# Layout changes of u and y in a state-space stage: two DRAM round trips against transfers within on-chip memory

## The reference, cut to what matters

```python
u = (h @ w_in).reshape(B, S, G, C)             # 64 groups of 16 channels
# per group: 64 complex states, x[s] = a * x[s-1] + bbar @ u[s]
y = einsum(x_re, c_re) - einsum(x_im, c_im) + d_skip * u
y = gelu(y)                                    # tanh form
val, gate = split(y @ w_glu)
h = h + val * sigmoid(gate)
```

## Time and profile before

| what | value |
|---|---|
| median of 3 runs | 1100.39 us (1098.67 to 1102.09) |
| profiled execution | 1102.55 us |
| its span, first to last instruction | 1100.7 us |
| TensorE matmuls busy | 1086.2 us (99%) |
| VectorE busy | 785.0 us (71%) |
| ScalarE busy | 476.1 us (43%) |
| GpSimd busy | 63.1 us (6%) |
| mean granted TensorE clock | 0.996 of full |

### The profile page before, as it was taken

One profiled execution on the slowest core, in us unless ns is written; L12 is line 12 of the kernel. 1 busy time (PEld: TensorE's weight loads), 2 busy tenths in 40 slices (PEclk: granted clock), 3 DMA queues, 4 the chain that ended last, 5 costly groups with the idle time before them and its releaser, 6 DMA issues.

```text
span 1100.7 us, 15912 instructions
## 1 busy us (share of the span) xinstructions
PE 1086.2 (99%) x6180; PEld 891.6 (81%) x6180; DVE 785.0 (71%) x1171; ACT 476.1 (43%) x744; POOL 63.1 (6%) x162
## 2 busy tenths in 40 slices
PE   9999999999999999999999989999999999999997
PEld 6778878888888888888887778888888888888886
DVE  6869848688787788978868866557774467655765
ACT  6557734444324543345452223344442244413453
POOL 1383031000000000000000000000000000000000
PEclk9999999999999999999999989999999999999999
DMA  7332214233233333333287843222223233235622
GB/s 234 108 112 81 68 38 135 77 115 133 97 128 122 115 115 110 124 113 124 86 277 218 247 140 118 96 96 96 96 96 101 99 101 100 79 114 138 144 88 91
DMA packets 81546, 131.25 MB, mean 119 GB/s; under 512 B 39040, under 2 KB 49024, under 8 KB 81472
## 3 DMA queue, kind: packets, MB, share of 16 engines
q1 hardware_dynamic: 71856, 123.69, 35.4%
q0 software_dynamic: 1152, 4.19, 1.1%
q10 hardware_dynamic: 8464, 2.36, 0.9%
HBM read 111.02 MB, written 14.88 MB: 114 GB/s over the span
## 4 chain that ended last, share of the span: by engine, by line
PE 92%; DVE 3%; DMA 2%; DVEq 1%; issue 1%; ACT 1%; SPq 0%; ACTq 0%
PE bank L1774 27%; PE bank L1775 27%; PE bank L1776 27%; PE bank L1980 2%; DMA ud_scratch<-UB 2%; PE bank L2077 1%; PE bank L2079 1%; PE bank L2078 1%; PE bank L1965 1%; DMA YB<-yd_scratch 1%; PE bank L2044 1%; PE bank L1846 1%; PE bank L1955 0%; PE bank L1953 0%; PE bank L1952 0%
## 5 line engine op out<-in xcount | busy, mean ns | idle before, releaser
L614 ACT ACTIVATE WH<-RAW 128x1024 fp32r<-128x1024 f32 (+1 forms) x169 | 175.8, 1042 | 343.0 <-PE bank L1776 328.1
L1774 PE MATMUL bank<-GH,WH 128*128 128x512 f32 x816 | 320.7, 393 | 0.0
L1776 PE MATMUL bank<-GH,WL 128*128 128x512 f32 x816 | 317.7, 389 | 0.0
L1775 PE MATMUL bank<-GL,WH 128*128 128x512 f32 x816 | 317.5, 389 | 0.0
L1032 DVE TENSOR_TENSOR WL<-RAW,WH 128x1024 fp32r<-128x1024 f32 (+1 forms) x169 | 202.8, 1201 | 35.5 <-ACT WH L614 35.0
L1774 PE MATMUL bank<-AH,WH 128*128 128x512 f32 x532 | 209.1, 393 | 4.3 <-DVE AL L1561 3.4
L1776 PE MATMUL bank<-AH,WL 128*128 128x512 f32 x532 | 207.4, 390 | 0.0
L1775 PE MATMUL bank<-AL,WH 128*128 128x512 f32 x532 | 207.3, 390 | 0.0
L1774 PEld LDWEIGHTS bank<-GH,WH 128*128 128x128 f32 x816 | 153.1, 188 | 32.6 <-issue 0.7
L1776 PEld LDWEIGHTS bank<-GH,WL 128*128 128x128 f32 x816 | 153.2, 188 | 32.2
L1775 PEld LDWEIGHTS bank<-GL,WH 128*128 128x128 f32 x816 | 153.2, 188 | 31.9 <-issue 0.7
(11 more groups left out here) (299 smaller groups left out, 1050.1 us busy)
## 6 DMA issues: line engine op xcount, KB each, us to landing
RAW<-in_w_up SPq DMA_DIRECT2D x88, 512.0 KB, 3.3
RAW<-in_w_dn SPq DMA_DIRECT2D x32, 512.0 KB, 3.2
RAW<-in_w_glu SPq DMA_DIRECT2D x16, 512.0 KB, 3.3
RAW<-in_w_dn SPq DMA_DIRECT2D x16, 384.0 KB, 3.1
RAW<-in_w_wo SPq DMA_DIRECT2D x8, 512.0 KB, 3.4
od_scratch<-OO SPq DMA_DIRECT2D x8, 512.0 KB, 3.3
kd_scratch<-KT SPq DMA_DIRECT2D x8, 512.0 KB, 4.5
O<-od_scratch POOLq DMA_DIRECT2D x8, 512.0 KB, 6.4
```

Source lines behind the costliest of these rows:

```text
L614: act_(w_hi(b)[:, :n], RAW[b % RW][:, :n], ACT.Copy).then_inc(s_hi, 1)
L1774: mm(out, wh, hi_[:, k, :], start=start, stop=False)
L1775: mm(out, wh, lo_[:, k, :], start=False, stop=False)
L1776: return mm(out, wl, hi_[:, k, :], start=False, stop=stop)
```

## The change

u and y change layout by transfers from on-chip memory to on-chip memory. One u tile goes in eight transfers, one for each group of 16 partitions (32 KB each), from UB into U2, issued by SyncE; one y tile goes in eight transfers from Y2 into YB, issued by ScalarE. The DRAM tensors UD and YD and the transfers on SyncE that read them are gone.

The inputs of the projection, GH and GL, are written in (step, chunk) order as they are made in `next_tile`, and so is RSTD in `rstd_copy`; these now read with a stride, and the multiply that makes UB doesn't.

The tables of tiles 5 and 7 get places of their own over ET, the input matrices of the first four tiles, and wait for inputs that have been made (`s_E`) instead of outputs. Table loads come one step earlier on SyncE for tiles 4, 5 and 7. In the order of TensorE the first two GLU blocks do three units each before the next tile's inputs, and their fourth units follow together; on VectorE one `y_lo` goes ahead of the last `states`.

```diff
-LAGS_AT = {2: 4, 3: 3, 5: 5, 6: 7}
+LAGS_AT = {1: 4, 3: 3, 4: 5, 5: 7}
...
+        for j in (5, 7):
+            TM[j], _ = place(f"TM{j}", [P, 2 * QJ, C * LQ], F32, A0 + 4096 * (j - 5))
+            O2[j], _ = place(f"O2{j}", [P, 2, QJ, C * LQ], F32, A0 + 4096 * (j - 4))
...
+        def timed(x, kind):
+            return x.rearrange("p (k s) -> p s k", s=LQ) if kind == "mix1" else x
+        def chunked(x, kind):
+            return x.rearrange("p (s k) -> p s k", k=NK) if kind == "mix1" else x
+        def group(i):
+            return slice(C * i, C * i + C)
+        def u_landed(j):
+            return s_ur[j % 3], 16 * GJ * (j // 3 + 1)
+        def y_landed(j):
+            return s_yr[j % 2], 16 * GJ * (j // 2 + 1)
...
             def u_out(j):
                 sp.wait_ge(s_ev, nth(FIRST["win"] + j))
-                sp.dma_start(UD[j], UB[j % 2][:]).then_inc(s_uw, 16)
-            def u_in(j):
                 if j >= 3:
                     sp.wait_ge(s_Y, j - 2)
-                sp.wait_ge(s_uw, 16 * (j + 1))
-                sp.dma_start(U2[j % 3][:], cmaj(UD[j])).then_inc(s_ur[j % 3], 16)
-            def y_in(j):
-                if j >= 2:
-                    sp.wait_ge(s_act, TILE0["y"] + j - 1)
-                sp.wait_ge(s_yw[j % 2], 16 * (j // 2 + 1))
-                sp.dma_start(YB[j % 2][:], YD[j]).then_inc(s_yr[j % 2], 16)
+                for i in range(GJ):
+                    sp.dma_start(U2[j % 3][:, i, :], UB[j % 2][group(i)]).then_inc(s_ur[j % 3], 16)
...
-                act_(GH[:, j, :], X[:, j, :], ACT.Identity, scale=gain(kind, j)).then_inc(s_thi, 1)
+                act_(chunked(GH[:, j, :], kind), timed(X[:, j, :], kind), ACT.Identity, scale=gain(kind, j)).then_inc(s_thi, 1)
...
             def y_out(j):
                 act.wait_ge(s_g, j + 1)
-                nc.scalar.dma_start(cmaj(YD[j]), Y2[j % 2][:]).then_inc(s_yw[j % 2], 16)
+                if j >= 2:
+                    act.wait_ge(s_act, TILE0["y"] + j - 1)
+                for i in range(GJ):
+                    nc.scalar.dma_start(YB[j % 2][group(i)], Y2[j % 2][:, i, :]).then_inc(s_yr[j % 2], 16)
...
-                v.tensor_tensor(UB[j % 2][:], bank[BANK[b]][:].rearrange("p (k s) -> p s k", s=LQ),
-                                RSTD[:].rearrange("p (k s) -> p s k", s=LQ), ALU.mult).then_inc(s_ev, 1)
+                v.tensor_tensor(UB[j % 2][:].rearrange("p s k -> p (s k)"), bank[BANK[b]][:], RSTD[:],
+                                ALU.mult).then_inc(s_ev, 1)
...
             states(NJ - 2)
+            y_lo(NJ - 4)
             states(NJ - 1)
-            y_lo(NJ - 4)
...
-            glu_part((0,), range(4))
+            glu_part((0,), range(3))
             inputs(NJ - 2)
             outputs(NJ - 3)
-            glu_part((1,), range(4))
+            glu_part((1,), range(3))
+            glu_part((0, 1), (3,))
             inputs(NJ - 1)
             outputs(NJ - 2)
```

More of the change, by code:

```diff
@@ L324, in build @@
             O2[i], at = place(f"O2{i}", [P, 2, QJ, C * LQ], F32, at)
-        for j, i in ((3, 0), (5, 1), (7, 0)):
-            TM[j], O2[j] = TM[i], O2[i]
+        TM[3], O2[3] = TM[0], O2[0]
+        for j in (5, 7):
+            TM[j], _ = place(f"TM{j}", [P, 2 * QJ, C * LQ], F32, A0 + 4096 * (j - 5))
+            O2[j], _ = place(f"O2{j}", [P, 2, QJ, C * LQ], F32, A0 + 4096 * (j - 4))
         for j in (2, 4, 6):
@@ L348, in build @@
         KD_ = nc.dram_tensor("kd_scratch", (NJ, P, LQ, C * LQ), F32, kind="Internal").ap()
-        UD = nc.dram_tensor("ud_scratch", (NJ, P, LQ, NK), F32, kind="Internal").ap()
         TD = nc.dram_tensor("td_scratch", (3, P, P), F32, kind="Internal").ap()
-        YD = nc.dram_tensor("yd_scratch", (NJ, P, LQ, NK), F32, kind="Internal").ap()
         s_raw = [sem(f"raw{i}_loaded") for i in range(RW)]
@@ L375, in build @@
         s_tmr, s_or = [sem(f"TM{j}_loaded") for j in range(NJ)], [sem(f"O{j}_loaded") for j in range(NJ)]
-        s_uw, s_ur = sem("ud_written"), [sem(f"U{i}_loaded") for i in range(3)]
+        s_ur = [sem(f"U{i}_spread") for i in range(3)]
         s_rt, s_E, s_X, s_Y, s_g = sem("RT"), sem("E"), sem("states"), sem("Y"), sem("gelu")
-        s_yw, s_yr = [sem("even_yd_written"), sem("odd_yd_written")], [sem("YB0_loaded"), sem("YB1_loaded")]
+        s_yr = [sem("YB0_spread"), sem("YB1_spread")]
         s_sig = sem("sigmoid")
@@ L534, in _, with place_free @@
                         lags(j)
-            def u_out(j):
-                sp.wait_ge(s_ev, nth(FIRST["win"] + j))
-                sp.dma_start(UD[j], UB[j % 2][:]).then_inc(s_uw, 16)
-            def u_in(j):
-                if j >= 3:
-                    sp.wait_ge(s_Y, j - 2)
-                sp.wait_ge(s_uw, 16 * (j + 1))
-                sp.dma_start(U2[j % 3][:], cmaj(UD[j])).then_inc(s_ur[j % 3], 16)
-            def y_in(j):
-                if j >= 2:
-                    sp.wait_ge(s_act, TILE0["y"] + j - 1)
-                sp.wait_ge(s_yw[j % 2], 16 * (j // 2 + 1))
-                sp.dma_start(YB[j % 2][:], YD[j]).then_inc(s_yr[j % 2], 16)
+            def place_free(j):
+                if j == 3:
+                    sp.wait_ge(s_Y, 1)
+                if j in (5, 7):
+                    sp.wait_ge(s_E, j - 3)
             def lags_in(j):
@@ L554, in lags_in @@
                 sp.wait_ge(s_kw, 16 * (j + 1))
-                if j in PLACE_FREE:
-                    sp.wait_ge(s_Y, PLACE_FREE[j])
+                place_free(j)
                 sp.dma_start(TM[j][:], bass.AP(k.tensor, k.offset, [[C * LQ, P], [C * LQ * P, GJ], [1, C * LQ]])
@@ L565, in _, with u_out @@
             lags_in(2)
+            def u_out(j):
+                sp.wait_ge(s_ev, nth(FIRST["win"] + j))
+                if j >= 3:
+                    sp.wait_ge(s_Y, j - 2)
+                for i in range(GJ):
+                    sp.dma_start(U2[j % 3][:, i, :], UB[j % 2][group(i)]).then_inc(s_ur[j % 3], 16)
             for t in range(NJ):
                 u_out(t)
-                u_in(t)
-                if t >= 3:
-                    y_in(t - 3)
                 load(FIRST["win"] + 5 + t)
@@ L573, in _ @@
                     lags_in(LAGS_AT[t])
-            for j in range(NJ - 3, NJ):
-                y_in(j)
             def x_rows_in(n):
@@ L948, in gelu @@
                 if j >= 2:
-                    act.wait_ge(s_yw[j % 2], 16 * (j // 2))
+                    act.wait_ge(*y_landed(j - 2))
                 for gi in range(2):
@@ L1058, in rstd_copy @@
                 dve.wait_ge(s_bc, NORMS.index(norm) + 1)
-                v.tensor_copy(dst[:], bank[3][:]).then_inc(s_rstd, 1)
+                kind = "mix1" if norm == "n_dn02" else None
+                v.tensor_copy(chunked(dst[:], kind), timed(bank[3][:], kind)).then_inc(s_rstd, 1)
                 v.drain()
@@ L1300, in next_tile @@
                 dve.wait_ge(s_thi, TILE0[key] + j + 1)
-                v.scalar_tensor_tensor(out=GL[:, j, :], in0=X[:, j, :], scalar=gain(kind, j),
-                                       in1=GH[:, j, :].bitcast(F32), op0=ALU.mult,
+                v.scalar_tensor_tensor(out=chunked(GL[:, j, :], kind), in0=timed(X[:, j, :], kind), scalar=gain(kind, j),
+                                       in1=chunked(GH[:, j, :].bitcast(F32), kind), op0=ALU.mult,
                                        op1=ALU.subtract).then_inc(s_act, 1)
@@ L1522, in u_out @@
                 if j >= 2:
-                    dve.wait_ge(s_uw, 16 * (j - 1))
-                v.tensor_tensor(UB[j % 2][:], bank[BANK[b]][:].rearrange("p (k s) -> p s k", s=LQ),
-                                RSTD[:].rearrange("p (k s) -> p s k", s=LQ), ALU.mult).then_inc(s_ev, 1)
+                    dve.wait_ge(*u_landed(j - 2))
+                v.tensor_tensor(UB[j % 2][:].rearrange("p s k -> p (s k)"), bank[BANK[b]][:], RSTD[:],
+                                ALU.mult).then_inc(s_ev, 1)
             def states(j):
@@ L1760, in _ @@
             fetch(2)
-            pool.wait_ge(s_ur[2], 16)
+            pool.wait_ge(*u_landed(1))
             fetch(4)
-            for j in (3, 5, 7):
-                pool.wait_ge(s_Y, PLACE_FREE[j])
+            pool.wait_ge(s_Y, 1)
+            fetch(3)
+            for j in (5, 7):
+                pool.wait_ge(s_E, j - 3)
                 fetch(j)
@@ L2085, in inputs @@
             def inputs(j):
-                pe.wait_ge(s_ur[j % 3], 16 * (j // 3 + 1))
+                pe.wait_ge(*u_landed(j))
                 if j == 0:
```

5 lines of the change are left out of this document (1 added, 4 removed).

## The result

The changed kernel takes 1112.63 us (median, 1109.70 to 1113.19) against 1100.30 of the kernel before in the same rounds: 1.0112 of its time [1.0096, 1.0128], 12.3 us slower where 4.7 less were forecast. Its profiled run has a span of 1110.8 us, 10.1 more than before.

What follows compares the result with a forecast made beforehand. TensorE was taken as the bound, busy 1086.2 of 1100.7 us. Of 8.95 us recoverable, new waits take 4.3, leaving a gain of 4.65 from a median of 1100.39: forecast 1095.7 us, range 1091 to 1100.

Steps and rivals of the forecast that it cites:

- 8.95 us recoverable: State-space stage: three TensorE waits, 6.06 us together, plus 2.89 of lowered clock after the long one, all to be given back.
- rival 4: VectorE sets the pace and landings stay behind weight loads, so other waits replace the old ones whole: about 1100; 9%.
- The price of an issue: Each small transfer inside SBUF holds its issuing engine 0.63 us, so a tile's eight issues hold it 5.05 us.
- Rival 1: Issues cost only 0.37 to 0.43 us, nearly all new waits vanish: about 1092; 18%.
- rival 5: The small transfers don't overlap: eight by 2.1 us is 16.8 a tile against 8.79, about 1150; 2%.
- 2.66 + 5.05 = 7.7 still fits below 8.79: ScalarE's own work plus eight y issues fits one tile's TensorE period, in us; delay of the weights behind costed at nothing.
- rival 3: ScalarE's issues exceed what fits in a period, above 0.77 us each: about 1119 at 1.058 an issue; 13%.
- The four new waits, 4.3: TensorE late in the stage: 1.8 for the last u, 2.1 at the end, 0.2 each for u(6) and states(7).
- The order (step, chunk): Ahead of the stage, dearer strided GH and GL go into 4.4 us of slack, costing nothing; UB's multiply saves 0.42 a tile.
- The moved table: TM of tile 4, one step earlier ahead of u of tile 2 on SyncE: a wait costed at nothing up to 1 us.
- No clock loss: No new wait in the stage is as long as the 3.42 us one that lowered the clock, so none was counted.
- Rival 2: A new wait at the stage's end lowers the clock again, costing 2.89 us: gain 1.9, about 1098.5; 16%.

Runs made afterwards that it cites:

- a3: The kernel before with only the two reorderings on TensorE and VectorE (GLU units, y_lo ahead of the last states); 1100.43 us, 1.0005.
- b3: a3 with only y moved inside on-chip memory, by eight transfers a tile issued by ScalarE; u still through DRAM; 1109.24 us, 1.0080.
- c3: b3 with each step's weight half and y copy put ahead of the eight issues on ScalarE; 1103.54 us, 1.0050.
- d1: The changed kernel with ScalarE's weight half and y copy put ahead of its eight issues; 1113.38 us, 1.0124.
- d4: c3 (u through DRAM) with the y transfers of tiles 5 to 7 issued by SyncE; 1100.97 us, 1.0005.
- d2: b4 with c3's order on ScalarE and the y transfers of tiles 5 to 7 issued by SyncE; 1102.61 us, 1.0033.
- b4: a3 with both u and y inside on-chip memory, natural order and tables as before; 1111.19 us, 1.0110.
- a1: The changed kernel with the table of tile 4 loaded one step later, as before; 1108.54 us, 1.0084.
- a4: The kernel before with only the (step, chunk) order, DRAM round trips kept; 1102.25 us, 1.0022.
- b1: a1 with GpSimd's table fetches held back to where they were in the kernel before; 1110.73 us, 1.0094.
- b2: a3 with only u moved inside on-chip memory by eight transfers a tile; y still through DRAM; 1101.05 us, 1.0013.
- a2: The changed kernel with GH, GL and RSTD in natural order and the strided multiply for UB; 1110.45 us, 1.0099.
- e2: The changed kernel with the edits of a1 and a2 and the y transfers of tiles 5 to 7 issued by SyncE; 1104.55 us, 1.0045.
- c2: a3 with ScalarE writing each y tile to DRAM in eight issues in place of one; 1102.91 us, 1.0023.
- c1: b4 with the y transfers issued by GpSimd instead of ScalarE; 1107.48 us, 1.0073.

## Why the prediction was wrong, by its own steps

- **8.95 us recoverable, "the three waits lose their causes": half right.** The AL wait went as foretold, but a3 shows that it goes by the reorder alone, and that this is worth nothing, since waits for u and XI come up behind it. Those were the next-late work, which the sum put at 4.3; without any change of transfers they are 4.7. This is rival 4 in kind: other waits replace the old ones.
- **The price of an issue: right at the median.** 0.60 and 0.62 against 0.63. But single issues of up to 1.76 us make a tile's run 5.6 on average, 5.0 to 6.6, where 5.05 was forecast. Rival 1 (cheap issues) falls, and so does rival 5: landings overlap, 2.4 us at the median with an issue every 0.6, not one after the other.
- **"2.66 + 5.05 = 7.7 still fits below 8.79", and the weights' delay at nothing: the step that failed.** b3 has only y's issues on ScalarE, and loses 8.2 us. The working asked only whether the sum fits into a period. It does (a period of the middle is still 8.8 us), so rival 3 isn't what happened. But ScalarE's work comes in an order, and what VectorE needs next came last: VectorE waited 8.3 us for the weight halves in the changed kernel, at most 4.0 at a time, near the "up to 5 us a tile" that was named for halves without cover. Their place behind the issues is worth about 3.3 in b3 (against c3, not quite clear of noise) and nothing by itself in the changed kernel (d1). Serving the last three tiles from SyncE gives 5.0 us (d4 against c3) or, with the weights' order, 8.5 (d2 against b4).
- **The four new waits, 4.3: near in total (5.2) by luck, and not where they were forecast.** In the changed kernel u of tile 7, put at 1.8, has 0.17, and AL of tile 6, put at 2.1, has none; u of tile 6 and the states of tile 7, put at 0.2 each, have 1.94 and 3.12. ScalarE was the late one at the end, as forecast, but the last states waited first: behind AL and AH for its issues. TensorE had lost time ahead of each forecast wait, 1.94 us before the first and 3.12 before the second. In a1, where these two are 0.77 and none, the forecast waits came, at 2.25 and 2.66: that part of the mechanism was right and its size a little small.
- **The order (step, chunk), "nothing": wrong, about 2 us by itself.** a4 loses 2.4 with it alone. The slack of 4.4 us was read at the last tile's square sum alone. Each of the eight tiles' GH and GL became dearer, and the step with the least slack was GM, 0.2 us, 26 us earlier. A new wait ahead of the first input block was named as the sign of this failure.
- **The moved table, "nothing up to 1 us": by the wait wrong, by the time about 3 and not clear of noise.** It is ahead of the u of tile 2 on SyncE's queue, and TensorE waits 4.76 us there, of which the later table takes back 1.56. b1 shows that more than this table is in play: holding GpSimd's fetches back moves the wait on by a tile. The DMA share stood above 1.0 in the wait for this u; that the landings are late because they share the DMA engines with the tables fits these rows, and no run has taken it apart.
- **No clock loss: wrong.** Rival 2 (16%) came true in kind: three waits, not one, were followed by a low clock, the shortest of them 1.94 us. The rule read from one wait (3.42 loses, 1.3 doesn't) was no rule about length: in b2 3.0 us lost nothing.
- **The sum.** 12.3 us: y through ScalarE is the largest part, 8.2 over a3 by itself. The table and the entrance can't be added to it: a1 and a2 give back 3.1 and 1.4 singly, but b4, which has neither, is as slow as the changed kernel. e2 gives back 7.4, with the end of y. u and y together cost 11.5, singly 0.9 and 8.2; the intervals don't settle whether they add. About half of y's 8.2 isn't explained by the hold, and why weights-first helps on the base but not in the changed kernel (d1) stays open too.

## What to carry to other kernels

A DMA issue is work of the engine that issues it: before moving transfers to an engine, list what stands behind them in its order and who waits for it, and don't be content that the sums fit into a period. Look for the smallest slack over every instance of a step that gets dearer, not at the last one, and for a queue that is passed, at what lands behind the moved load. When a wait is taken away, test the removal alone first: a3 showed that the target of this change was worth nothing by itself.

## What was not expected of the hardware

- An issue by ScalarE costs 0.366 us towards DRAM when one transfer stands alone. With eight in a row (c2) it took 0.46 at the median but up to 1.65, 0.58 on average; inside on-chip memory (changed kernel) 0.62 at the median, up to 1.64, 0.70 on average. What makes the long ones no run shows.
- GpSimd's issues take 0.53 us, but eleven stalls between them took 24.2 us in c1, up to 5.8 each.
- The copy of RSTD out of its matmul bank (PSUM) takes 0.69 us with a stride as without one, where the strided GL went from 0.75 to 1.22.
- A landing of 32 KB took 2.4 us at the median, but up to 8.0 where a weight block and a table were issued just ahead.
- The granted clock fell after a wait of 1.94 us in one kernel and not after one of 3.0 in another. What decides it no run here shows.
